# Freeing two PSUM banks earlier and reordering the decode-state stretch of a hybrid decoder step

## What is computed

```python
proj = a @ w_in                                  # a = rmsnorm(h); 1024 -> z 512, xbc 1024, dt 8, u 512, v 512
xbc  = silu(conv4(xbc))                          # causal convolution of width 4, then split in xs, B, C
y, state = ssd_chunked(xs, dt, A, B, C, state0)  # decayed sums over tokens; 8 heads of 64, 128 states, 2 groups
y    = rms(y * silu(z)) ;  m = rmsnorm(gelu(u) * chunk_mix(layernorm(gelu(v))))
h    = h + concat(y, m) @ w_out
h    = h + moe(rmsnorm(h))                       # top 4 of 32 experts, 1024 -> 2048 -> 1024
h    = h + (p @ w_ple) * sigmoid(rmsnorm(h) @ w_gate) ;  out = rmsnorm(h)
```

## Time and profile before

| what | value |
|---|---|
| median of 3 runs | 1163.11 us (1161.58 to 1163.46) |
| the profiled execution's own time | 1164.74 us |
| its span, first to last instruction | 1163.0 us |
| PE busy with matmuls | 1096.3 us, 94% |
| DVE, ACT, GpSimd busy | 388.0, 142.8, 33.3 us |
| mean granted TensorE clock | 0.989 of full |
| moved by DMA | 433.88 MB, mean 373 GB/s |

### The profile page before, as it was taken

One profiled execution on the slowest core, in us unless ns is written; L12 is line 12 of the kernel. 1 busy time (PEld: TensorE's weight loads), 2 busy tenths in 40 slices (PEclk: granted clock), 3 DMA queues, 4 the chain that ended last, 5 costly groups with the idle time before them and its releaser, 6 DMA issues.

```text
span 1163.0 us, 16351 instructions
## 1 busy us (share of the span) xinstructions
PE 1096.3 (94%) x6471; PEld 446.0 (38%) x6475; DVE 388.0 (33%) x988; ACT 142.8 (12%) x320; POOL 33.3 (3%) x81
## 2 busy tenths in 40 slices
PE   8699999999999999989898899999999898989896
PEld 4465445334343333333333233334333333333332
DVE  3756657233223131313131123222313131313155
ACT  2232113101010001000000100001000000000022
POOL 2300121000000000000000000000000000000000
PEclk9799999999999999999999899999999999999999
DMA  7830693999999999999999999999999999999941
GB/s 266 290 149 9 220 405 118 429 428 427 427 427 427 426 429 429 428 429 428 428 428 428 428 427 427 428 425 431 429 428 429 428 429 428 428 429 428 417 165 41
DMA packets 42334, 433.88 MB, mean 373 GB/s; under 512 B 6691, under 2 KB 7851, under 8 KB 17720
## 3 DMA queue, kind: packets, MB, share of 16 engines
q1 hardware_dynamic: 40224, 428.74, 88.1%
q0 software_dynamic: 1488, 4.48, 1.2%
q10 hardware_dynamic: 584, 0.14, 0.1%
HBM read 429.04 MB, written 4.30 MB: 373 GB/s over the span
## 4 chain that ended last, share of the span: by engine, by line
PE 67%; DMA 27%; DVE 3%; ACT 1%; issue 1%; ACTq 0%; SPq 0%; DVEq 0%
PE bank L1016 27%; DMA ring<-in_w_up_dram 25%; PE bank L1062 12%; PE bank L1000 6%; PE bank L623 5%; PE bank L725 4%; PE bank L984 3%; PE bank L656 2%; DMA ring<-in_w_in_dram 1%; PE bank L1046 1%; DVE arena L1477 1%; PE bank L1091 1%; PE bank L908 1%; PE bank L605 1%; PE bank L981 1%
## 5 line engine op out<-in xcount | busy, mean ns | idle before, releaser
L1016 PE MATMUL bank<-ring,aT 128*64 128x512 f32 x1536 | 348.7, 599 | 27.9 <-DMA ring<-in_w_up_dram 27.6
L1016 PEld LDWEIGHTS bank<-ring,aT 128*64 128x64 f32 x1536 | 106.6, 137 | 254.3 <-issue 200.5
L1062 PE MATMUL bank<-ring,arena 128*64 128x512 f32 x768 | 169.6, 594 | 0.2
L1887 DVE TENSOR_TENSOR h<-h,bank 128x512 f32<-128x512 f32 (+1 forms) x96 | 65.7, 684 | 179.4 <-PE bank L1000 177.1
L1016 PE MATMUL bank<-arena,aT 128*64 128x512 f32 x512 | 115.7, 596 | 3.4 <-DMA arena<-in_w_up_dram 3.4
L1904 DVE TENSOR_SCALAR arena<-bank 128x256 f32<-128x256 f32 x64 | 27.2, 425 | 236.6 <-PE bank L1016 235.4
L1913 DVE COPY aT<-bank 64x512 f32<-64x512 f32 x32 | 22.2, 694 | 245.0 <-PE bank L1062 245.0
L1333 ACT ACTIVATE arena<-arena 128x256 f32<-128x256 f32 x64 | 26.7, 417 | 549.8 <-DVE arena L1904 549.7
L1062 PEld LDWEIGHTS bank<-ring,arena 128*64 128x64 f32 x768 | 53.8, 137 | 100.9 <-issue 98.2
L1000 PE MATMUL bank<-aT,arena 128*128 128x512 f32 (+1 forms) x192 | 83.5, 622 | 1.4 <-DVE aT L1913 0.9
L1016 PEld LDWEIGHTS bank<-arena,aT 128*64 128x64 f32 x512 | 35.3, 136 | 77.7 <-issue 69.8
(11 more groups left out here) (331 smaller groups left out, 741.7 us busy)
## 6 DMA issues: line engine op xcount, KB each, us to landing
ring<-in_w_up_dram SPq DMA_DIRECT2D x96, 2048.0 KB, 32.6
ring<-in_w_down_dram SPq DMA_DIRECT2D x48, 2048.0 KB, 33.3
arena<-in_w_up_dram SPq DMA_DIRECT2D x32, 2048.0 KB, 33.0
arena<-in_w_down_dram SPq DMA_DIRECT2D x16, 2048.0 KB, 33.6
ring<-in_w_in_dram SPq DMA_DIRECT2D x3, 2048.0 KB, 13.1
ring<-in_w_in_dram SPq DMA_DIRECT2D x4, 1024.0 KB, 8.7
ring<-in_w_out_dram SPq DMA_DIRECT2D x1, 4096.0 KB, 13.9
ring<-in_w_ple_gate_dram SPq DMA_DIRECT2D x2, 2048.0 KB, 13.5
```

The source lines that it names most:

```text
L1016: mm = pe.matmul(bank[n][CAP * hf:CAP * hf + CAP, :], xT[:, odd, 2 * j + a, :], up_cols(x, j, a, hf, n), start=False, stop=(j == 3 and a = ...
L1062: mm = pe.matmul(bank[4][CAP * hf:CAP * hf + CAP, :], actT[:, b, t, :], tile_of(x, UP_TILES + t)[:, 1024 * b + 512 * hf:1024 * b + 512 * h ...
L1887: tt(part, part, bank[5 + j % 2][at:at + ROWS[c], :], ALU.add).then_inc(s_free[j % 2], 1)
```

## The change

Three things are changed. Nothing that is computed changes, and the number of instructions on each engine stays as it is.

1. ACT reads `decs` between xbc tiles 2 and 3, no longer after the decay tables.
2. DVE reads `acb2` ahead of the convolution of tile 2, no longer behind it.
3. On PE, the steps of the second z projection stand ahead of the transposes of the decode states, two and two; the product of a pair of sequences (`decode_rows`) comes one turn later, and that of the last pair behind the products `st`. The banks of that stretch are given by hand, from which those of later jobs that take their turn shift too: `zuv2` comes to lie in the bank of `("yd", 2)`, and the first four `ns` in those of `("z", 1)`, `("yd", 0)`, `("yd", 1)` and `yo1`.

```diff
@@ plan_psum @@
-    jobs += [("yos", 4, 6), (("z", 1), 1, 7)]
-    jobs += [(("h0T", b), 1, b % 6) for b in range(B_S)]
-    jobs += [(("st", c), 1, None) for c in range(2)]
-    jobs += [(("yd", 0), 1, None), (("yd", 1), 1, None), ("yo1", 1, None), (("yd", 2), 1, None)]
+    jobs += [("yos", 4, 6), (("z", 1), 1, 1)]
+    jobs += [(("h0T", b), 1, (2, 3, 4, 5)) for b in range(B_S)]
+    jobs += [(("st", c), 1, (7, 0)) for c in range(2)]
+    jobs += [(("yd", 0), 1, 2), (("yd", 1), 1, 3), ("yo1", 1, 4), (("yd", 2), 1, 5)]
@@ PE @@
-            h0_rows(0)
-            h0_rows(1)
-            for b in range(0, B_S, 2):
-                if b + 2 < B_S:
-                    h0_rows(b + 2)
-                    h0_rows(b + 3)
-                project_step("z", 0, 1, b)
-                project_step("z", 0, 1, b + 1)
+            def decode_rows(b):
+
                 stored(pe, ("h0T", b))
                 stored(pe, ("h0T", b + 1))
                 for n in range(2):
...
+            for b in range(0, B_S, 2):
+                project_step("z", 0, 1, b)
+                project_step("z", 0, 1, b + 1)
+                h0_rows(b)
+                h0_rows(b + 1)
+                if b:
+                    decode_rows(b - 2)
+
             for c in range(2):
                 stored(pe, ("btm", c))
...
                 close_bank(("st", c), mm)
+            decode_rows(B_S - 2)
@@ ACT @@
-            for t in (1, 2, 3):
-                store_xbc(t)
+            store_xbc(1)
+            store_xbc(2)
+            o = filled(act, "decs")
+            act.activation(decs[:, :, :].rearrange("p t b -> p (t b)"), o[:, 0:32], ACT.Exp).then_inc(freed("decs"), 1)
+            store_xbc(3)
...
             act.activation(lmat_s, lmat_s, ACT.Exp).then_inc(S["lexp"], 1)
-            o = filled(act, "decs")
-            act.activation(decs[:, :, :].rearrange("p t b -> p (t b)"), o[:, 0:32], ACT.Exp).then_inc(freed("decs"), 1)
@@ DVE @@
-            convolve(2)
             o = filled(dve, "acb2")
             for hh in range(HEADS):
                 stt(lmat_s[:, hh, :], o[0:T_S, hh * T_S:(hh + 1) * T_S], acum[0:T_S, 2, hh:hh + 1], negm_s[:, :],
                     ALU.subtract, ALU.add).then_inc(freed("acb2"), 1)
+            convolve(2)
             convolve(3)
```

## The result

| | before | after |
|---|---|---|
| median of 4 runs | 1163.28 us (1161.58 to 1164.06) | 1154.41 us (1154.32 to 1155.94) |
| the profiled execution's own time | 1164.74 us | 1155.94 us |
| its span | 1163.0 us | 1154.2 us |
| mean granted clock | 0.989 | 0.994 |

The change is faster: the ratio is 0.9931, with a 95% interval of 0.9916 to 0.9946. On the median from which the forecast was made, 1163.11, that is 1155.1 us, outside its range (1148.8 to 1154.6) by half a microsecond. The sign was right and the forecast gain too large: 11.9 us were forecast, and 8 to 9 were measured.

A forecast was written before the change was run, and what follows sets the result against it. The prediction took the experts' fixed-rate w_up stream, started by expert 0, as the bound, so earlier gains pass on. Early reads (-13.2 us) and decode-state reordering (+1.3) sum to -11.9: 1151.2 us from 1163.11, range 1148.8 to 1154.6.

The forecast's parts named there:

- The view of the bound: Experts end by a fixed-rate w_up stream; whatever moves expert 0's start moves the end by as much.
- Part 1: Early reads of `decs` and `acb2`: 10.2 us ahead of bT plus 3.1 for the clock, taken as 13.2 gained.
- the tiles at full clock: Four xbc tiles behind bT: 15.5 us at full clock in place of 18.59, a gain of 3.1 us.
- The margins worked out for tile 5 and the last SiLU: Slack behind the early reads: 0.5 us for tile 5's acb bank, 1.7 us for the last SiLU.
- Part 2: New order and banks of the decode states: 1.5 us gained, 2.8 us new wait, net loss 1.3 us.
- DVE's chain: DVE's work from yos to its read of yd 2: 9.33 us, making `zuv2` wait until 109.0 (old time scale).
- the rival by which it would run shorter: DVE's chain ahead of `zuv2` shortens, returning up to 2.8 us: 1148.4 to 1150.2 us, chance 0.10.
- the 2.8 us of rest that were expected of PE: PE's new wait ahead of `zuv2` for DVE's read of yd 2, partly already before the later first `ns`.
- the term for the clock in part 2: Clock fall in the waits around `ns` and `zuv2`: nothing in the forecast time, only a bound and rival.
- the sum: Whole change: -13.2 + 1.3 = -11.9 us, giving 1151.2 us from the median 1163.11.
- the new waits draw the clock down: Rival: waits before `ns` and `zuv2` lower the clock, costing 1.5 to 3 us; 1152.7 to 1154.2, chance 0.16.
- The second rival: Something else late among the early reads and tiles, or a clock fall there, costs up to 2 us; chance 0.09.

The follow-up runs named there:

- e5: The whole change, with the last pair's `decode_rows` product moved ahead of the two `st`; 1150.00 us, ratio 0.9889.
- the two fillers: The whole change plus products nobody reads: eleven around the first four `ns` (1152.53 us), or four behind the fourth only (1152.57 us).
- e3: The whole change with other banks, so neither the first four `ns` nor `zuv2` lie in a bank DVE reads late; 1148.56 us, ratio 0.9870.
- e1: The early reads of `decs` and `acb2` alone, applied to the kernel before; 1151.63 us, ratio 0.9904.
- e2: The new PE order and banks of the decode states alone, applied to the kernel before; 1167.26 us, ratio 1.0034.
- e0: The changed kernel again, no edit; 1153.04 us, ratio 0.9914.
- e9: The whole change with two banks exchanged: `zuv2` in that of `yos`, v 0 in that of yd 2; 1153.33 us, ratio 0.9905.
- look_a: The changed kernel once more, no edit; 1153.70 us, ratio 0.9911.
- look_b: The changed kernel once more, no edit; 1154.68 us, ratio 0.9920.
- e6: The kernel before with `decs` read early on ACT, `acb2` still read late; 1152.41 us, ratio 0.9902.
- e7: The early reads and the banks of e3, with PE's order of the decode states as before the change; 1149.05 us, ratio 0.9875.

## Why the prediction was right and wrong

**The view of the bound was right.** The last leg is 966.0 to 966.7 us in eleven of the fourteen traces, wherever expert 0 starts between 181 and 199 us. The start of the stream moves the end one to one. The exceptions are e5, where the clock also fell at 1107 us, and the two fillers, which are 1.0 to 1.9 us shorter for a reason that I did not find.

**Part 1 was right.** 10.2 us were forecast in front of bT and 10.3 are there without the clock's fall (19.38 - 9.08); 3.1 for the tiles at full clock and 2.83 (18.70 - 15.87) are there. The margins worked out for tile 5 and the last SiLU held in the changed kernel's traces: PE rests nowhere between wT 0 and rep. That of tile 5, 0.5 us, is as narrow as it looked: e3 overran it by 0.4. e1 has all of it alone.

**Part 2 was right in its waits.** zuv2 waits for the read of yd 2, and the leg is 1.51 us longer, where 1.3 were forecast. DVE's chain from yos to that read takes 9.33 us after the change as before it (87.19 to 96.52), so the rival by which it would run shorter is out. e5 moved the start of DVE's chain and with it the wait; e3 took the wait away and got 2.9 us, where 2.8 were forecast for it. The wait doesn't make the change slower than before, but it makes part 2 a loss (e2). One detail was off: of the 2.8 us of rest that were expected of PE, only 1.01 is shown at full clock (e0), as the late ns fill the time.

**The step that failed** is the term for the clock in part 2, which the sum puts at nothing. The prediction has it only as a rival, "the new waits draw the clock down" (the first in its list, though the sentence on the rule calls it the second), with a chance of 0.16, and its reason against was that there are short products between the rests and that PE had been at work without a stop. The runs showed that this does not hold the clock: of the four traces of the changed kernel and that of e2 the fall came in four, and in e9 and in the changed kernel's first trace it came while PE was shown busy without a gap. Its price was bounded from 1.5 to 3 us, and 1.27 to 2.50 were measured. With its 2.5 us the sum is 1153.7; the median over all 14 executions of the changed kernel (after, e0, look_a and look_b) is 1154.1. The rival was the likely case and should have been the forecast. The rule of the Trainium skill that was set against part 2 ("TensorE: Matmul & The Clock Gate", section "A second HAM failure mode: psum-queue depth-cycling") names short idle times of PE between groups of products, for banks gone round in turn, as what makes the clock swing. The traces agree with it in part: waits for banks bring the clock down, but it fell once and came back once in each of these stretches, and in e9 no idle time of PE is shown among the ns ahead of it, only 0.81 and 0.43 us of its weight loads.

**What no term of the sum had** is the fall behind the small products at 37 us, 1.69 us where it comes. The second rival names "a clock that falls in part 1 after all" in half a sentence, without this place. It came in four of fourteen traces, among them the first of the changed kernel, which fits with that execution taking 1155.94 while the other three stood at 1154.4. PE's instructions up to there are the same in all variants, it comes with early reads (e1, e5, e6) and stays away from others with the same reads (e3, e7), and in e1 and e6 it comes without part 2. That it didn't come in the one trace of before and in e2 may be chance; this stays open. Further scatter, up to 1.9 us, is in the first leg, 32.75 to 34.66, ahead of anything that was edited.

**Chance had a part in the number.** The fall around zuv2 alone leaves the sum inside the range (1153.7). The ratios of the same kernel in e0, look_a and look_b put it at 1153.1, 1152.8 and 1153.8 from the same 1163.11, all inside; the first measurement, 1155.1, lies outside. The step above is wrong either way.

## What to carry to other kernels

When jobs take turns in a few PSUM banks, the bank of each big product is a choice about whom it waits for: look up which reader frees it, and where that reader stands in its own queue, before the order of the writers is changed. Here other banks for the first ns and zuv2 were worth 2.9 us and the new order 0.2. And price a short wait of TensorE as the wait plus a possible fall of the clock over what stands behind it; two waits of 0.8 and 0.4 us among products of 32 rows were enough (e9).

## What the runs showed of the hardware

- The clock fell in stretches in which PE's record has no gap: in e9 at 92.3 us, where only its weight loads waited, 0.81 and 0.43 us, and products of 32 rows came two by two in place of eight side by side; and in four traces near 37 us, where its longest gap was 0.25 us and its products were small. With a rest of 1.01 us ahead of zuv2 the clock stayed up in e0 and e5. So neither a busy share of 1.00 nor a short gap tells whether it stays up.
- Whether it falls differs from one execution to the next of the same kernel, and so does the price: 0, 1.27, 1.67 and 2.50 us for the same waits. One trace can't tell whether a stretch is safe; the same legs over several traces can.
- Where neither the clock nor the waits differ, the legs repeat to 0.03 us over kernels and executions (15.87, 36.44, 88.82). That makes them a finer measure than the medians, whose intervals here are some 3 to 4.5 us wide.
